# Two VectorE steps of each attention unit change places: the maximum of the newest scores ahead of the lower part of the older transposed probabilities

## The reference

```python
hn = rms_norm(x, norm_attn); proj = hn @ w_in          # queries, keys, values, latents
oa = block_attention(qa, ka, va, 1/sqrt(64))            # 8 heads, 2 shared keys, width 64
ob = block_attention(qm, km, vb, 1/sqrt(96))            # 8 heads from latents, width 64 + 32
x  = x + concat(rms_norm(oa), rms_norm(ob)) @ w_o
x  = x + expert_choice_moe(rms_norm(x), ...)            # 16 experts, 64 tokens of each set
# block_attention: p = softmax(scale * q @ k.T); o = p @ v, for every head
```

## Time and profile before

| | |
|---|---|
| median of 3 runs | 1083.67 us (1082.73 to 1084.68) |
| the profiled execution | 1086.1 us; its span, first to last instruction, 1083.7 us |
| busy over the span | PE 1044.8 us (96%), DVE 886.0 (82%), ACT 775.3 (72%), POOL 423.3 (39%) |
| granted TensorE clock | 0.986 of full speed on average, 1.00 all through attention |

### The profile page before, as it was taken

How to read it: one execution, slowest core, us unless ns; L and a number is a source line. 1 busy time by engine, 2 the same in 40 slices (tenths; PEclk the granted TensorE clock), 3 DMA queues, 4 the chain that set the end, 5 groups by cost and what they waited for, 6 DMA issues and landing times.

```text
span 1083.7 us, 16970 instructions
## 1 busy us (share of the span) xinstructions
PE 1044.8 (96%) x5689; PEld 896.7 (83%) x5689; DVE 886.0 (82%) x1147; ACT 775.3 (72%) x1095; POOL 423.3 (39%) x394
## 2 busy tenths in 40 slices
PE   8999999999999999998699999999999999999995
PEld 7999978999889987887578888888888888888884
DVE  6787669989999843338899999999999999999991
ACT  7655569888998843344577877877878878788771
POOL 2466576111358502334524432344323444234101
PEclk9999999999999999999799999999999999999998
DMA  8232050010211348741799999999999999999982
GB/s 305 79 116 102 1 197 1 2 41 20 98 41 40 98 109 263 225 164 79 235 417 378 398 400 400 400 421 400 401 400 400 413 408 401 400 400 406 415 310 39
DMA packets 77936, 266.05 MB, mean 245 GB/s; under 512 B 11249, under 2 KB 13516, under 8 KB 77628
## 3 DMA queue, kind: packets, MB, share of 16 engines
q1 hardware_dynamic: 69776, 239.68, 56.9%
q0 software_dynamic: 8048, 25.68, 8.3%
q10 hardware_dynamic: 60, 0.01, 0.0%
HBM read 239.07 MB, written 26.28 MB: 245 GB/s over the span
## 4 chain that ended last, share of the span: by engine, by line
PE 48%; DVE 2%; DMA 1%; issue 1%; ACT 0%; POOLq 0%; POOL 0%; DVEq 0%; ACTq 0%
PE ps L2003 10%; PE ps L2005 10%; PE ps L2004 10%; PE ps L2017 5%; PE ps L2019 5%; PE ps L2018 5%; PE ps L1980 1%; DMA xe<-h,idxT 1%; DMA out<-y,give 1%; DVE lo L2171 0%; DVE idx L1776 0%; DVE affT L1785 0%; DVE gates L1771 0%; ACT hi L2093 0%; POOLq L2274 0%
## 5 line engine op out<-in xcount | busy, mean ns | idle before, releaser
L2171 DVE TENSOR_TENSOR lo<-raw,hi 128x2048 fp32r<-128x2048 f32 x191 | 430.0, 2285 | 32.3 <-ACT hi L2093 32.0
L2093 ACT ACTIVATE hi<-raw 128x2048 fp32r<-128x2048 f32 x192 | 364.6, 1918 | 70.0 <-PE ps L2005 57.3
L2003 PE MATMUL ps<-hi,xehi 128*128 128x512 f32 x480 | 188.3, 392 | 1.3 <-DVE h L2193 1.0
L2005 PE MATMUL ps<-hi,xelo 128*128 128x512 f32 x480 | 186.9, 389 | 0.0
L2004 PE MATMUL ps<-lo,xehi 128*128 128x512 f32 x480 | 186.8, 389 | 0.0
L1939 POOL DMA_INDIRECT xe<-h,take x60 | 111.1, 1851 | 25.1 <-issue 13.7
L2003 PEld LDWEIGHTS ps<-hi,xehi 128*128 128x128 f32 x480 | 90.1, 188 | 20.2 <-issue 1.4
L2005 PEld LDWEIGHTS ps<-hi,xelo 128*128 128x128 f32 x480 | 90.1, 188 | 18.8
L2004 PEld LDWEIGHTS ps<-lo,xehi 128*128 128x128 f32 x480 | 90.2, 188 | 18.1
L1934 POOL COPY take<-idx 128x4 uint32 (+1 forms) x15 | 29.0, 1930 | 193.7 <-DVE xt L2187 187.4
L1361 DVE TENSOR_TENSOR probTlo<-ps,probThi 128x512 fp32r<-128x512 f32 x128 | 87.8, 686 | 12.1 <-ACT probThi L1318 10.0
(11 more groups left out here) (302 smaller groups left out, 2192.3 us busy)
## 6 DMA issues: line engine op xcount, KB each, us to landing
raw<-in_w_down SPq DMA_DIRECT2D x64, 1024.0 KB, 10.0
raw<-in_w_gate SPq DMA_DIRECT2D x60, 1024.0 KB, 9.7
raw<-in_w_up SPq DMA_DIRECT2D x60, 1024.0 KB, 9.3
w_raw<-in_w_in SPq DMA_DIRECT2D x8, 592.0 KB, 9.0
x<-in_x SPq DMA_DIRECT2D x8, 512.0 KB, 3.7
woraw<-in_w_o SPq DMA_DIRECT2D x4, 1024.0 KB, 5.1
o<-attention_out SPq DMA_DIRECT2D x8, 512.0 KB, 4.4
xr<-in_x SPq DMA_DIRECT2D x8, 512.0 KB, 7.0
```

The costliest lines, as they stand in the source:

```text
L2003: pe.matmul(ps[:, dst[n], :], rowhi[:, c, :], hi[w][:, cols], start=c == 0, stop=False)
L2005: last = pe.matmul(ps[:, dst[n], :], rowlo[:, c, :], hi[w][:, cols], start=False, stop=c == KD - 1)
L2093: act.activation(hi[s][:], raw[s][:], ACT.Copy).then_inc(hi_done, 1)
L2171: dve.tensor_tensor(lo[s][:], raw[s][:], hi[s][:].bitcast(F32), ALU.subtract).then_inc(lo_done, 1)
```

## The change

In each turn DVE first waits for and takes the maximum of unit u, and then the low part of unit u - 4. Nothing else differs: the same instructions with the same operands, semaphores and counts, and the programs of the other engines are untouched. The other work of the turn on DVE still comes after both.

```diff
         for u in range(NU + STEPS):
+            if u < NU:
+                dve.wait_ge(score_ready, u + 1)
+                dve.tensor_reduce(att["nmax"][:, u:u + 1], ps[:, S_BANKS[u % 3], :], AX.X, ALU.max,
+                                  negate=True).then_inc(max_done, 1)
             if 0 <= u - 4 < NU:
                 v = u - 4
                 dve.wait_ge(pthi_done, v + 1)
                 cols = pair_cols(v)
                 dve.tensor_tensor(ptlo[v // 2 % 2][:, :, cols], ps[:, T_BANKS[v % 2], :].rearrange("p (a c) -> p a c", a=TS),
                                   pthi[v // 2 % 2][:, :, cols].bitcast(F32), ALU.subtract).then_inc(ptlo_done, 1)
-            if u < NU:
-                dve.wait_ge(score_ready, u + 1)
-                dve.tensor_reduce(att["nmax"][:, u:u + 1], ps[:, S_BANKS[u % 3], :], AX.X, ALU.max,
-                                  negate=True).then_inc(max_done, 1)
             for kind, g in due.get(u, []):
                 prepare(kind, g)
```

## The result

The changed kernel takes 1096.67 us (median of 4 runs, 1096.29 to 1098.52), the kernel before 1083.26 in the same comparison (1082.73 to 1084.68): 1.0125 times, 95% interval 1.0108 to 1.0143, or 13.4 us slower. Forecast were 1095.2 us and +11.5. The span of the profiled execution is 1096.7 us, against 1083.7.

A forecast was written before the change was run, and what follows sets the result against it. PE was taken to set attention's pace, with DVE close behind. Grouped heads 6.05 and latent heads 5.6 sum to 11.6, taken as 11.5, on 1083.67: 1095.2 us; forecast 1092.5 to 1098.5 (0.66), 8-in-10 range 1089.0 to 1100.0.

The forecast's parts named there:

- The chain: From the end of scores(u) through maximum and low part to the start of T(u-2): 1.48 us.
- The rival of a chain 0.15 longer each time: Restart after waits costs more in some 38 chains, adding 5.7 us: 1101 us, chance 0.13.
- Even units have cover: For even u eight value products precede T(u-2), so PE needs 1.7 us or more and the chain is hidden.
- The start: Attention to unit 17: new waits mostly run inside PE's old wait for DVE's statistics, +0.4 us.
- Grouped heads from unit 17 on: Odd units wait for the chain: +3.4 us in three plain periods, +2.25 in periods with a key to prepare.
- Latent heads: +0.6 us from first odd units after a key, +4.4 from six two-key turns, +0.6 from turn 60; together 5.6.
- ACT off the path: In attention, ACT's exponentials and copies fit within 3.51 us per pair, so they do not delay PE.
- One for one to the end: Output projection, routing and experts start from attention's output, so attention's 11.5 us delay passes to the end unchanged.
- PE full in the latent heads: PE is busy 20.00 of 20 us, hiding nothing; the rival that room hides the latent part, 1089.7 us, got 0.13.
- The longer DRAIN: If DVE starts were 0.68 us apart, not 0.60, some 35 chains grow 0.08 each and the sum becomes about 14.3.
- Faster: Rival: earlier maxima fill DVE's 9.6 us of waits and win PE's idle time in attention: 1080.1 us, chance 0.04.
- The signs: Expected after-profile: grouped stretches 8 to 10% PE idle, probTlo waits 10 us or more, attention ending near 402 us.

The follow-up runs named there:

- The half maximum: Both orders with the maximum over only the first 256 of 512 scores: changed kernel 1087.09 us (1.0028), kernel before 1080.47 us (0.9969).
- with even turns only: Maximum first only in even turns, odd turns in the order of the kernel before: 1089.28 us, 1.0040 times the kernel before.
- the copies that take this away: Changed kernel plus a one-column DVE copy behind each prepared part of a grouped head: 1106.64 us in one run, attention 240.69 us.
- the kernel with the key before the maximum: Maximum first only in turns 2, 6, 10, ..., and in turns 12 and 76 taken last, behind the key: 1083.27 us, 0.9994 times the kernel before.
- the run with the latent heads alone: New order only in turns of the latent heads (units 32 to 63, 96 to 127): 1091.08 us, 1.0055 times the kernel before.

## Why the prediction was right

- **The mechanism** was right. T(u-2) waits for lo(u-4), now behind scores(u) and max(u). The chain is 1.47 us (predicted 1.48), the pair of grouped units 3.50 (3.51), both measured at unit 65, and the first odd latent unit (33) has 1.47 in place of 1.41. In all six turns with two latent keys it is 4.23, as predicted; with a grouped key (turns 60 and 76) 4.20 for 4.08. The half maximum shows that the chain's length sets the loss. The rival of a chain 0.15 longer each time falls by the 1.47.
- **Even units have cover**: right in the changed kernel, where from unit 5 on T(u-2) waits for its low part for one even u (84) and for 42 odd ones. It is not right of any order: with even turns only, DVE is late behind a head's output and grouped even turns pay some tenths. That even turns with two keys pay on a second path was seen, as 0.5 us; it measured 0.50.
- **The sizes.** From unit 3 on, 13.09 us against 11.6: each part was put too low, by 0.4 to 0.5 us. The start: 0.89 against 0.4; I had followed a queue that is behind with other work. Grouped heads from unit 17 on: 1.95 from 17 to 33 and 4.14 from 65 to 97, 6.1 against 5.65. There the low parts that start late (0.12 us in units 19, 67, 83, and again behind a grouped key) were missing; with the copies that take this away, the same two stretches add 5.6. Latent heads: 3.42 + 2.69 = 6.1 against 5.6; each turn with two keys lost 0.76 (0.73 said), turn 60 0.74 (0.6 said), and unit 125 another 0.08 that was not counted. The rest are hundredths in many places: a first transpose after a wait takes 0.63 instead of 0.60.
- **ACT off the path**: yes here, by the 2.35 us and more that the exponentials are ahead; the kernel with the key before the maximum shows where it would come on.
- **One for one to the end**: right within 0.7 us. The 0.7 is a clock (-1.46) and a gather (+0.78), which happened to cancel in part; without that luck the span would fit less well.
- **PE full in the latent heads**: yes. Nothing of the 6 us was hidden, though weight loads were busy for 18.33 of 20 us only. The Trainium skill, Perfetto Trace Analysis, section Identifying the Most-Contended Engine, judges TensorE's headroom by the share of peak arithmetic and the weight loads' busy time. It speaks of how close a kernel is to the roofline; as a measure of the room for new waits it would have left 1.7 us in each 20 there, and the run with the latent heads alone decides against that reading.
- **The longer DRAIN**: DVE starts follow at 0.60 to 0.61 us, with 0.73 in a few places, so not 0.68 everywhere. With 0.68 the sum was 14.3, a little nearer to 13.1 than 11.6 is, by coincidence: the chain of unit 65 would be 1.56 and is 1.47, and the slower places carry only 0.42 of the missing 1.5 us. The prediction took half of what the Trainium skill states in the section The DRAIN you can't avoid of VectorE: DVE Perf Modes, which adds that a next operation that is not held starts earlier; the 0.60 us agrees with that.
- **Faster**: the waits that the change removes, 9.6 us of DVE, are in fact gone (0.8 left), and the kernel that moves the maximum only in turns 2, 6, 10, ... has 1.1 us less of attention.
- **The signs**: PE is 7.6% idle in the stretch from 280 to 300 us (8 to 10% said). The list of waits shows 7.6 us in 13 places for T behind probTlo, where 10 us or more in 30 to 40 places was said; the other places stand there under the weight loads, and the timeline has 42.

## What to carry to other kernels

In a software pipeline with in-order engines, ask of each hand-over what the busiest engine issues next and how long it has until then: here 0.75, 1.2 or 1.4 to 1.5 us in most odd turns and 1.7 and more in the rest and in even ones. The sum of the queue's instructions between the event and that start is the price, and what exceeds the cover is lost in every round. A wait that the slower engine shows (9.6 us here) is not a gain to be had; move an instruction ahead only in the turns where nothing that the busiest engine needs next stands behind it, and look for the second consumer (here the keys for the queries' transposes), and for turns in which the slower engine is late, before calling the rest free.

## What was not expected of the hardware

- A low part that reads SBUF from partition 0, where DVE's last read of SBUF started at partition 64, starts 0.72 or 0.73 us after the maximum in front of it instead of 0.60 or 0.61; a 0.16 us copy that reads from partition 0 in an idle moment takes this away.
- PE's granted clock fell after a 2.20 us wait for a transfer in one trace and stayed after a 2.09 us wait in the other; the same work then took 5.03 and 3.57 us.
- The experts' stage is close to its transfers: one execution showed 77 us of ACT's waits for weights where another kernel with the same experts' code had 0.9, and its experts took 7.4 us longer. Its cause stays open.
